# Hybrid attention and recurrence block with 32 experts: expert blocks gather, add to and scatter the output rows in place of a combine stage

## What is computed

```python
h = h + concat([o_a, o_b]) @ w_out
h = h + hier_moe(rms_norm(h, ln2_g), ...)

def hier_moe(t, ...):          # t: 2048 x 1024
    # one of 4 groups per token, then 2 of the group's 8 experts
    gate = p_group * top_p / sum(top_p)
    # every expert's tokens are put into blocks of 128 slots, the rest of a block is padding
    expert_block = lambda xb, e: (silu(xb @ w_gate[e]) * (xb @ w_up[e])) @ w_down[e]
    y = einsum('nkd,nk->nd', y_slots, gate)   # the two experts' rows of each token, weighted
```

## Time and profile before

| what | us |
|---|---|
| median of 3 runs (lowest, highest) | 3657.55 (3646.26, 3658.22) |
| the profiled execution | 3652.28 |
| its span, first to last instruction | 3650.6 |
| PE busy in the span | 3159.7 |
| DVE busy | 1523.2 |
| ACT busy | 1121.5 |
| POOL busy | 183.0 |

### The profile page before, as it was taken

The page is one execution under the profiler, slowest core; times in us unless marked ns, Lnnn a source line. Parts: engine busy times, 40 slices in busy tenths (PEclk is TensorE's granted clock), DMA queues, the critical chain, the costliest instruction groups (busy, mean ns, idle before and its releaser), DMA issues. The chain is left out here.

```text
span 3650.6 us, 62481 instructions
## 1 busy us (share of the span) xinstructions
PE 3159.7 (87%) x24000; PEld 2099.9 (58%) x24001; DVE 1523.2 (42%) x3383; ACT 1121.5 (31%) x2480; POOL 183.0 (5%) x200
## 2 busy tenths in 40 slices
PE   5999999999788888788888699937999999999970
PEld 5778777777555555788888455513444444444430
DVE  3676666766567776233333477720000000000013
ACT  2333333333377777222222133300111111111110
POOL 0000000000000000000000000031000000000013
PEclk9999999999799999899999899958999999999985
DMA  5121111111211100322222533254855556877548
GB/s 207 53 66 58 56 50 63 63 54 60 78 44 45 45 9 9 98 68 68 68 75 61 189 128 133 92 157 174 322 185 194 184 184 223 319 260 264 198 168 309
DMA packets 214391, 463.54 MB, mean 127 GB/s; under 512 B 20353, under 2 KB 86017, under 8 KB 212609
## 3 DMA queue, kind: packets, MB, share of 16 engines
q1 hardware_dynamic: 185616, 385.06, 30.2%
q0 software_dynamic: 19456, 41.99, 4.1%
q10 hardware_dynamic: 9072, 33.03, 2.5%
HBM read 343.01 MB, written 117.03 MB: 126 GB/s over the span
## 5 line engine op out<-in xcount | busy, mean ns | idle before, releaser
L285 PE MATMUL pj_big<-pj_xnT,pj_w_in 128*128 128x256 f32 x2816 | 645.7, 386 | 10.7 <-issue 9.3
L285 PEld LDWEIGHTS pj_big<-pj_xnT,pj_w_in 128*128 128x128 f32 x2816 | 545.4, 194 | 95.9 <-issue 16.7
L1743 DVE TENSOR_TENSOR ex_hh<-ex_sg,ex_pu 128x128 f32<-128x128 f32 x94 | 35.3, 418 | 943.5 <-PE ex_pu L1682 943.5
L1682 PE MATMUL ex_pg<-ex_wg,ex_xT 128*128 128x512 f32 x752 | 334.2, 598 | 9.3 <-DMA ex_wd<-in_w_exp_down 7.9
L1697 PE MATMUL ex_py<-ex_wd,ex_hT 128*128 128x512 f32 x752 | 331.1, 593 | 0.0
L1682 PE MATMUL ex_pu<-ex_wu,ex_xT 128*128 128x512 f32 x752 | 330.4, 592 | 0.0
L1682 PEld LDWEIGHTS ex_pg<-ex_wg,ex_xT 128*128 128x128 f32 x752 | 142.8, 191 | 194.0 <-issue 194.0
L1682 PEld LDWEIGHTS ex_pu<-ex_wu,ex_xT 128*128 128x128 f32 x752 | 142.9, 190 | 179.8 <-issue 179.8
L1215 PE MATMUL mg_po<-mg_w_out,mg_mix 128*128 128x512 f32 x512 | 230.3, 609 | 4.1 <-DMA mg_w_out<-in_w_out 2.8
L706 ACT ACTIVATE at_e<-at_sc,at_nmx 128x512 f32<-128x512 f32 (+3 forms) x320 | 196.8, 621 | 115.0 <-DVE at_nmx L745 114.8
L1697 PEld LDWEIGHTS ex_py<-ex_wd,ex_hT 128*128 128x128 f32 x752 | 139.0, 190 | 157.4 <-issue 157.4
(11 more groups left out here) (268 smaller groups left out, 4765.3 us busy)
## 6 DMA issues: line engine op xcount, KB each, us to landing
ex_wg<-in_w_exp_gate SPq DMA_DIRECT2D x32, 2048.0 KB, 9.5
ex_wu<-in_w_exp_up SPq DMA_DIRECT2D x32, 2048.0 KB, 14.5
ex_wd<-in_w_exp_down SPq DMA_DIRECT2D x32, 2048.0 KB, 18.5
slots_s<-ex_yb ACTq DMA_DIRECT2D x47, 512.0 KB, 4.9
chunks_s<-pj_st SPq DMA_DIRECT2D x32, 642.0 KB, 4.0
rw_raw<-chunks_s SPq DMA_DIRECT2D x32, 642.0 KB, 4.9
slots_s<-rw_zero SPq DMA_DIRECT2D x32, 512.0 KB, 5.9
pj_xt<-in_x SPq DMA_DIRECT2D x20, 512.0 KB, 3.7
```

What stands on the lines that cost most here:

```text
L285: ins = pe.matmul(out, lhs, rhs, start=(k == 0), stop=(k == KC - 1))
L1682: ins = pe.matmul(out[:, :], xT[:, k, :], w[:, k, :], start=(k == 0), stop=(k == KC - 1))
```

## The change

The expert stage writes the layer's output itself, and there is no combine stage.

- `merge` stores `h` straight into the output tensor. The scratch tensors `h`, `slots` and `slot_tok` are gone, and so is the clearing of `slots` in `recur`.
- `dispatch` scatters a record of two numbers per slot, the token number and its gate (as floats), into `table`, which is first filled with the token number 2048 and the gate 0. There are 66 x 128 records. The same 32 indirect DMAs do it, with 8 bytes where there were 4. A few small DVE operations are added: they round the number of blocks up to an even one, and the last expert gets the block that this may add.
- The number of an expert in the order of work is changed by the constant `c_eiota`: position 4i+q is expert 8q+i, so four neighbours belong to four groups, and no token is in two of them.
- `experts`: SP first loads the whole table into SBUF (`tab`, record of slot t of block b on partition t) in two DMAs, blocks 0 to 3 and 4 to 64, then the constants. DVE clears three tiles first, and POOL waits for that, then issues two small DMAs that only count up a semaphore.
- For a block, POOL copies the token numbers from `tab` and gathers the rows of `hn`, and also gathers the same rows of the output (`acc`, two buffers). An index beyond the last token is left out by the DMA. DVE, and no longer ACT, takes the block's output from PSUM: `yb = py * gate + acc`. POOL scatters `yb` to the rows of the output. Block b+1's `acc` is gathered after block b-1's scatter has been issued; a scatter waits for the one before it to have landed.
- The gate and up weights are loaded when the expert two before has finished its last up product, the down weights when it has finished its last down product, and PE waits for the two groups apart.
- ACT, DVE and POOL loop over pairs of blocks; PE over experts as before.

```diff
@@ recur
-            def clear(n):
-                sp.dma_start(dr["slots"][(NE + n) * P:(NE + n + 1) * P, :], zero[:, :]).then_inc(o_zero, 16)
...
@@ merge
-                    sp.dma_start(dr["h"][rows, :], hb[:, t, :]).then_inc(o_h[t], 16)
+                    sp.dma_start(io["out"][0, rows, :], hb[:, t, :]).then_inc(o_h[t], 16)
@@ dispatch
+            sp.wait_ge(s_blank, 2)
+            sp.dma_start(dr["table"].rearrange("(p n) a -> p n a", p=P), blank[:, :, :]).then_inc(s_blank, 16)
             ahead(sp)
...
+            pool.memset(blank[:, :, :].rearrange("p n a -> p (n a)"), 0.0).then_inc(s_blank, 1)
+            pool.memset(blank[:, :, 0], float(S)).then_inc(s_blank, 1)
+            pool.tensor_copy(rec[:, :, :, 0], wide(ids[:, :], 2)).then_inc(s_rec, 1)
...
-                    pool.indirect_dma_start(dr["slot_tok"], bass.IndirectOffsetOnAxis(keep["slot"][:, t, n:n + 1], 0),
-                                            ids[:, t:t + 1], None).then_inc(o_sc, 16)
+                    pool.indirect_dma_start(dr["table"], bass.IndirectOffsetOnAxis(keep["slot"][:, t, n:n + 1], 0),
+                                            rec[:, t, n, :], None).then_inc(o_sc, 16)
...
+            dve.tensor_copy(rec[:, :, :, 1], keep["gate"][:, :, :]).then_inc(s_rec, 1)
...
+            chain(dve.tensor_copy(odd[:, 0:1], ends[:, NE - 1:NE]))
+            chain(dve.tensor_scalar(odd[:, 1:2], odd[:, 0:1], 1, None, ALU.bitwise_and))
+            chain(dve.tensor_copy(oddf[:, :], odd[:, 1:2]))
+            chain(dve.tensor_tensor(oddf[:, :], oddf[:, :], ends[:, NE - 1:NE], ALU.add))
+            dve.tensor_scalar(keep["turns"][:, :], oddf[:, :], 0.5, -1.0, ALU.mult, ALU.add)
...
+            chain(dve.tensor_tensor(oddf[:, :], oddf[:, :], ends[:, NE - 1:NE], ALU.subtract))
+            dve.tensor_copy(keep["blocks"][:, 0, NE - 1:NE], oddf[:, :])
@@ experts
         @block.sync
         def _(sp):
+            for s0, b0, b1 in ((0, 0, 4), (1, 4, NB + 1)):
+                src = dr["table"][b0 * BT:b1 * BT, :].rearrange("(b t) w -> t b w", t=BT)
+                sp.dma_start(tab[:, b0:b1, :], src).then_inc(s_tab[s0], 16)
             sp.dma_start(ident[:, :], io["c_ident"]).then_inc(s_const, 16)
             sp.dma_start(cols[:, :], io["cols"]).then_inc(s_const, 16)
-            with sp.Fori(0, NE // 2 - 1) as i:
-                for x in range(2):
-                    sp.wait_ge(s_done, 2 * i + x + 1)
-                    weights(sp, bass.ds(2 * i + x + 2, 1), x)
+            def refill(i, q):
+                n, first = blocks_of(sp, 4 * i + q - 2)
+                sp.wait_ge(s_pu, first + n)
+                weights_in(sp, bass.ds(EPG * q + i, 1), q % 2)
+                sp.wait_ge(s_py, first + n)
+                weights_out(sp, bass.ds(EPG * q + i, 1), q % 2)
...
         @block.gpsimd
+            def rows_x():
+                pool.indirect_dma_start(xb[:, :], None, dr["hn"], bass.IndirectOffsetOnAxis(idx[:, 0:1], 0),
+                                        bounds_check=LAST, oob_is_err=False).then_inc(s_x, 16)
+            def rows_acc(x):
+                pool.indirect_dma_start(acc[x][:, :], None, io["out"][0], bass.IndirectOffsetOnAxis(idx[:, 0:1], 0),
+                                        bounds_check=LAST, oob_is_err=False).then_inc(s_acc[x], 16)
+            def scatter(b, x):
+                pool.wait_ge(o_y, 16 * b + 32)
+                pool.sem_inc(s_apart, 1)
+                pool.tensor_copy(idy[:, :], tab[:, bass.ds(b, 1), 0]).then_inc(s_idy, 1)
+                pool.wait_ge(s_idy, b + 1)
+                pool.sem_inc(s_apart, 1)
+                pool.wait_ge(s_yb, b + 2)
+                pool.sem_inc(s_apart, 1)
+                pool.indirect_dma_start(io["out"][0], bass.IndirectOffsetOnAxis(idy[:, 0:1], 0), yb[x][:, :], None,
+                                        bounds_check=LAST, oob_is_err=False).then_inc(o_y, 16)
+            def next_x(b):
+                pool.tensor_copy(idx[:, :], tab[:, bass.ds(b + 1, 1), 0]).then_inc(s_idx, 1)
+                pool.wait_ge(s_idx, b + 2)
+                pool.sem_inc(s_apart, 1)
                 pool.wait_ge(s_px, b + 1)
                 pool.sem_inc(s_apart, 1)
+                rows_x()
...
+            pool.wait_ge(s_clear, 1)
+            for n in range(2):
+                pool.dma_start(dr["spare"][n], acc[0][:, 0:1]).then_inc(o_y, 16)
...
+            with pool.Fori(0, more) as i:
+                for n in range(2):
+                    b, x = 2 * i + 1 + n, 1 - n
+                    pool.wait_ge(s_x, 16 * b + 16)
+                    pool.wait_ge(s_acc[x], 16 * (i + n) + 16)
+                    pool.sem_inc(s_apart, 1)
+                    next_x(below(b, NB - 2))
+                    scatter(below(2 * i + n, NB - 2), 1 - x)
+                    rows_acc(1 - x)
...
         @block.tensor
+                pe.wait_ge(s_wo[x], 16 * i + 16)
                 pe.wait_ge(s_yb, b + 1)
...
         @block.scalar
-                act.activation(yb[:, :], py[:, :, :].rearrange("p a n -> p (a n)"), ACT.Copy).then_inc(s_yb, 1)
-                act.dma_start(dr["slots"][bass.ds(b * P, P), :], yb[:, :]).then_inc(o_y, 16)
...
         @block.vector
+            for buf in acc:
+                dve.memset(buf[:, :], 0.0)
+            dve.memset(xb[:, :], 0.0).then_inc(s_clear, 1)
...
+                    dve.wait_ge(s_px, b + 2)
+                    copy_x()
+                    dve.wait_ge(s_py, b + 1)
+                    dve.wait_ge(s_acc[x], 16 * i + 16)
+                    dve.wait_ge(o_y, 16 * b + 16)
+                    dve.scalar_tensor_tensor(yb[x][:, :], py[:, :, :].rearrange("p a n -> p (a n)"), tab[:, bass.ds(b, 1), 1], acc[x][:, :],
+                                             ALU.mult, ALU.add).then_inc(s_yb, 1)
-    with ExitStack() as ctx:
-        m = Pool(nc, ctx, "cb")
...
```

More of the change, by code:

```diff
@@ L1594, in experts @@
         hT = m.sb("hT", [P, DE // P, P])
-        yb = m.sb("yb", [P, D])
+        acc = [m.sb(f"acc{x}", [P, D]) for x in range(2)]
+        yb = [m.sb(f"yb{x}", [P, D]) for x in range(2)]
         px = m.ps("px", [P, KC, P])
@@ L1601, in experts @@
         s_const = m.sem("const")
-        s_done = m.sem("done")
-        s_idx = m.sem("idx_ld")
+        s_clear = m.sem("clear")
+        s_tab = [m.sem(f"tab{n}") for n in range(2)]
+        s_idx = m.sem("idx_done")
+        s_idy = m.sem("idy_done")
         s_x = m.sem("x")
+        s_acc = [m.sem(f"acc_ld{x}") for x in range(2)]
         s_px = m.sem("px_done")
@@ L1622, in experts, with pairs @@
         PARTS = (slice(0, P), slice(P, DE))
-        def turns(eng, body, before=None, past=None):
-            with eng.Fori(0, NE // 2) as i:
-                for x in range(2):
-                    n = eng.value_load(keep["blocks"][0:1, 0, bass.ds(2 * i + x, 1)], min_val=1, max_val=NT)
-                    first = eng.value_load(keep["blocks"][0:1, 1, bass.ds(2 * i + x, 1)], min_val=0, max_val=NB - 2)
-                    if before:
-                        before(i, x)
-                    with eng.Fori(0, n) as j:
-                        body(nc.s_assert_within(first + j, 0, NB - 2, skip_runtime_bounds_check_because="the experts' blocks add up to less than NB"), x)
-                    if past:
-                        past()
+        def pairs(eng):
+            return eng.value_load(keep["turns"][0:1, 0:1], min_val=NE // 2 - 1, max_val=NB // 2 - 1)
@@ L1639, in _, with blocks_of, below @@
+        def blocks_of(eng, v):
+            n = eng.value_load(keep["blocks"][0:1, 0, bass.ds(v, 1)], min_val=1, max_val=S // BT + 1)
+            first = eng.value_load(keep["blocks"][0:1, 1, bass.ds(v, 1)], min_val=0, max_val=NB - 1)
+            return n, first
+        def below(b, top):
+            return nc.s_assert_within(b, 0, top, skip_runtime_bounds_check_because="the experts' blocks add up to at most NB")
         @block.sync
         def _(sp):
+            for s0, b0, b1 in ((0, 0, 4), (1, 4, NB + 1)):
+                src = dr["table"][b0 * BT:b1 * BT, :].rearrange("(b t) w -> t b w", t=BT)
+                sp.dma_start(tab[:, b0:b1, :], src).then_inc(s_tab[s0], 16)
@@ L1665, in _ @@
+            b = below(2 * more + 1, NB - 1)
+            pool.wait_ge(s_x, 32 * more + 32)
+            pool.wait_ge(s_acc[1], 16 * more + 16)
+            pool.sem_inc(s_apart, 1)
+            next_x(b)
+            scatter(below(2 * more, NB - 2), 0)
+            scatter(b, 1)
+            pool.wait_ge(o_y, 32 * more + 64)
+            pool.wait_ge(s_x, 32 * more + 48)
+            pool.sem_inc(s_apart, 1)
         @block.tensor
```

198 lines of the change are left out of this document (80 added, 118 removed).

## The result

The changed kernel takes 3529.95 us (median of 4 runs, 3526.01 to 3533.0). The kernel before, run beside it, takes 3657.14 us. The ratio is 0.9658, 95% interval 0.9637 to 0.9679: faster by 3.4%, 127 us. The forecast was 3568 us with a range of 3553 to 3591, so the direction was right and the gain 38 us larger than forecast, outside the range.

What follows compares the result with a forecast made beforehand. PE was taken to bound the expert stage. The terms -114.1 + 5.2 + 22.1 - 7.9 + 6.6 = -88.1 us gave 3564.2 us from the profiled execution, 3569.4 from the median; 3568 us was taken, range 3553 to 3591.

Steps and rivals of the forecast that it cites:

- dispatch part: Dispatch: DVE's added small steps cost +1.5 us; larger scatters, and the clearing of `slots` gone from the recurrence, count nothing.
- Combine stage and tail: End of kernel: the combine stage's 114.1 us go whole; a new tail costs about 5.2 us, up to 10.5.
- One block more: Expert stage: 47 blocks round up to 48, and PE runs the padding block like any other, +22.08 us.
- Rival E: Expert stage: the padding block is nearly free, as PE pauses elsewhere or blocks are counted otherwise; 3546 us, chance 0.02.
- Weights earlier: Expert stage: gate and up asked for about 8 us sooner, down needed later, so PE's waits for weights go, -7.9 us.
- Accumulation rows: Expert stage: `acc` gathers, scatters and their waits on DVE and POOL cost nothing while PE covers them.
- rival D: Expert stage: POOL's queue closes a ring, PE waits once gathers take over 16 us; slower, 3748 us at 18; chance 0.03.
- Rival C: Expert stage: DMA engines bound one-block experts, up to +31 us, and the 7.9 us stay; up to 3607 us, chance 0.08.
- Entry: Start of the expert stage: PE starts at 2489 in place of 2482.4, +6.6 us.
- path (b): Expert entry, SP: constants queue behind the table's small elements, 10.7 us at 20.6 ns each; there at about 2489.
- path (a): Expert entry, POOL: DVE's clearing, two small issues, index copy, then a 4.8 us gather; rows at about 2486, +3.6 us alone.
- Rival B: Expert entry: the table's read is dear, 55 ns a packet, PE starts 25 us late; 3586 us, chance 0.13.

Runs made afterwards that it cites:

- Experiments 1: Changed kernel with the 32 clearing stores of 512 KB put back into the recurrence, to a scratch tensor nobody reads: 3571.53 us, ratio 0.9766.
- 2: Kernel before with its 32 clearing stores moved from the recurrence into the attention stage: 3623.88 us, ratio 0.9909.
- 3: Changed kernel with clearing stores back in the recurrence, 28 of 32 cut into four of 128 KB at four points of a chunk: 3539.27 us, ratio 0.968.
- 4: Changed kernel with two clearing stores of 512 KB behind each chunk's load in the recurrence: 3574.7 us, ratio 0.9774.
- Experiment 10: Changed kernel with PE's work of the 48th, padding block left out, PE only counting up its semaphores: 3514.9 us, ratio 0.9609.
- experiments 8: Changed kernel with gate and up weights asked for only after the last down product of the expert two before: 3536.0 us, one run.
- 9: Changed kernel with all weights asked for after the last down product, and PE waiting for all three tensors at once: 3541.79 us, one run.
- experiment 7: Changed kernel with POOL's two counting DMAs made loads of 128 rows of 512 bytes, issued before its wait for the clearing: 3528.23 us, ratio 0.9643.
- experiment 5: Changed kernel with the expert stage's two constants ahead of the table in SP's queue: 3535.54 us, one run.

## Why the prediction was right or wrong

**The step that failed** is the last sentence of the dispatch part: "The clearing of `slots` in the recurrence and POOL's memset there are not waited for", priced at "nothing for both, and no gain". It was worth 32.6 us of the 35.1 us by which the profiled execution beat the sum. Experiments 1, 2 and 3 settle that the clearing is the cause: put back alone it costs 31.9 us, taken from the kernel before it gives 33 us, and cut into four it costs 3 to 6 us. That PE stands because a piece of its program is late rests on the traces: PE stops in mid-run with nothing shown to wait for; the pauses fall behind a load and a clearing; they go when the burst is cut; and in the kernel before and experiments 1 and 4 all 47 pauses over 0.9 us end 1.2 to 1.6 us after a packet of queue 8. That queue 8 carries PE's program, and not another engine's, is read from this and from its name; no run changed it by itself. The pauses explain 28.1 - 3.3 = 24.8 us of idle time. PE's longer busy time at the lower clock behind some of them adds 9.7 us, and its waits for other engines came out 2 us shorter, which leaves the 32.6. The mistake in the reading was to ask only who waits for the store, and not what shares the DMA engines with it. The row that would have warned, 28.1 us of "issue" before PE's products in the recurrence, was in the trace and was not read. The Trainium skill, page "Runtime: NRT & Kernel Launch", section "Instruction fetch mechanics", says that an engine's program is refilled in 16 KiB blocks and that crossing such a boundary is "mostly hidden". The trace agrees on the size (110 packets, 1.80 MB) and bounds the second: hidden while only the chunk loads ran beside it (3.3 us of pauses), and 28.1 us of pauses with a store behind each load.

**Combine stage and tail: right.** -105.9 us against -108.9. The landing of the last scatter and POOL's late wake made the tail 8.2 us, inside the 5.2 to 10.5 given.

**One block more: right.** Experiment 10 takes 22.0 us from the stretch, against 22.08 forecast. Rival E is out. Passing the block by signals gives only 16 us of the 22, as the scatters then lie in the tail; a kernel without the 48th block was not tried.

**Weights earlier: right in size, half in cause.** The 7.9 us are gone. The forecast named both the earlier request and the later need for the down weights, and gave the credit to the 8 us of slack from the request; experiments 8 and 9 show that the later wait for the down weights is enough alone. The whole stretch came out 2.8 us below forecast: PE's busy time rose by 19.3 us (1042.77 to 1062.05), not by 22.1. The trace does not tell where these 2.8 us were before.

**Accumulation rows: right.** `acc` rows land 7.9 us after issue (median), rows of `hn` 6.5, and POOL's longest wait for `acc` was 10.9 us against the 16 us from which rival D begins. PE waited for none of it. (One figure of rival D is a slip: by its own terms, 2L + 3.5 - 36 us in each of 48 blocks, L = 18 gives 3736 us and not 3748.)

**Rival C: not seen.** No wait for weights, and gate, up and down land after 8.7, 13.7 and 12.7 us (medians), far from 22.

**Entry: the size was near, by luck, the reason wrong.** +9.7 us with the dispatch stage, against +6.6. Dispatch itself is 0.2 us longer and not 1.5 (66.4 against 66.2 us until the expert stage's first DMA), so the entry alone took 9.5 us more. The forecast let path (b) bind, constants behind a dear table. In fact path (a) bound, as in the forecast's smaller case, but with a gather of 12.0 us where "4.8 us ... with 1 us for the traffic beside it" had stood. The two small DMAs ahead of it were counted by their issue, 0.6 us each, and not by what they may do to a gather behind them. How they do it stays open: their own packets are over at 2441.5 us, 2 us before the gather's first one at 2443.5. Path (b) is real but came second: with the gather back at 4.8 us, PE waits for the constants (experiment 7). The DMA queues in the middle of the slow gather, after, 2444 to 2449 us, show its packets alone: 31 packets of 4 KB took 76.1% of 16 engines' 5 us, about 2 us each, at 26 GB/s:

```profile
DMA packets 56, 0.13 MB, mean 26 GB/s; under 512 B 25, under 2 KB 25, under 8 KB 56
...
q0 software_dynamic: 31, 0.13, 76.1%
```

Rival B did not occur. The table's 7808 elements landed after 7.1 us in experiment 7, between the 5.5 us estimated from the page's figure and the 10.7 us taken; in the changed kernel 8640 packets of SP's queue (the row below, 2436 to 2454 us; 8320 of them are the table's elements, one packet each) kept 16 engines busy for 30.7% of 18 us, about 10 ns each of one engine's time. The Trainium skill, page "DMA: Bandwidth & Descriptors", section "Measured (HBM→SBUF, 128 partitions, SWDGE, issued from GpSimd)", gives about 10.5 ns a packet as the floor, but it gets it by dividing the 0.67 us of a whole small transfer by its 64 packets. The two figures are near each other and measure different things, so the forecast's use of it as an engine's time per packet is not borne out by the page, only by this row. The price of 20.6 ns from the earlier trace rows was too high: it was that of a lone 4-byte load.

```profile
q1 hardware_dynamic: 8640, 0.16, 30.7%
```

**The first stretch.** -6.0 us that no part of the change touches. It varies by as much among the other kernels, so it is counted as scatter. PE does the same 6320 products in it with 7.4 us more of busy time before (1297.6 against 1290.2), and the granted clock stood at 0.5 for 101 us of it before and 81 us after. What makes the clock fall more often in one run than in another stays open.

**The range** allowed for costs of unknown size in the expert stage alone. Every term that the forecast put at "nothing" outside it went in with no spread.

## What to carry to other kernels

A store whose result nobody needs is not always free beside an engine whose program is written out over thousands of instructions: look at that engine's "issue" waits and at the instruction queue before pricing its removal or addition at nothing, and cut large background transfers into pieces, or move them to a stage that loops. Split a joint wait by when each tensor is first used; here that alone hid late weights. Suspect tiny DMAs ahead of a gather in the same queue, and try them earlier or as whole rows.

## What the runs showed that I had not expected

- A 512 KB store behind a 642 KB load cost about 1 us per chunk (32 us in 32 chunks) though nothing reads what it writes; in four pieces of 128 KB 0.1 to 0.2 us; two of them 1.25 us (40 us in 32), little more than one.
- PE goes on 1.2 to 1.6 us after an instruction packet has landed, in every pause over 0.9 us of the recurrence, and some of these pauses of 1 to 4 us are followed by 3.4 to 6.8 us at half the granted clock.
- Two stores of 128 elements of 4 bytes ahead of it let a gather of 128 rows of 4 KB land in 12 us; two loads of 128 rows of 512 bytes let it land in 4.8 us, though 8000 small elements were read beside it. The second pair was also issued 3.9 us ahead of the gather in place of 2.3, so whether size, direction or distance in time is the reason was not separated.
- SP's issue of the 64 KB identity matrix takes 4.1 us behind the table's 7808 elements (4.5 us in experiment 7) and 0.34 us ahead of them (experiment 5), and the issue of the next constant waits for it.
